# Hybrid attention/mLSTM trunk: the norm between the layers spread over ACT, POOL and DVE, the gates and the first unit of layer 1 run by blocks together, and the spill of x moved in the first stage

## What is computed

```python
for l in range(2):
    sh, sc, gt = split(silu(c) @ w_ada[l] + b_ada[l])         # adaLN, per sequence
    h = rmsnorm(x, g_pre[l]) * (1 + sc) + sh
    y = attention_branch(h) if l == 0 else mlstm_branch(h)     # both end in ... @ w_out
    x = x + gt * rmsnorm(y, g_post[l])
```

## Time and profile before

| | us |
|---|---|
| median of 3 runs | 2308.17 (2307.28 to 2312.15) |
| the profiled execution | 2304.96 |
| its span in the profile | 2303.4 |
| PE busy | 2189.6 |
| DVE busy | 951.0 |
| ACT busy | 687.5 |
| POOL busy | 65.2 |

### The profile page before, as it was taken

How to read it: one execution, slowest core, us unless ns; L and a number is a source line. 1 busy time by engine, 2 the same in 40 slices (tenths; PEclk the granted TensorE clock), 3 DMA queues, 4 the chain that set the end, 5 groups by cost and what they waited for, 6 DMA issues and landing times.

```text
span 2303.4 us, 40939 instructions
## 1 busy us (share of the span) xinstructions
PE 2189.6 (95%) x17200; PEld 1995.8 (87%) x17200; DVE 951.0 (41%) x1393; ACT 687.5 (30%) x1124; POOL 65.2 (3%) x108
## 2 busy tenths in 40 slices
PE   5889999999999999996999999999999999989996
PEld 3479998999999977784899999999999999977995
DVE  1423545636456421117543434334343434361225
ACT  2323443534344321123322222222222222232222
POOL 1000000000000000000000000000000000000000
PEclk9889999999999999997999999999999999999998
DMA  8983313222222399973356656784557568829522
GB/s 324 351 282 86 87 56 86 64 59 74 77 56 58 121 313 294 295 233 103 83 87 105 81 106 76 106 85 98 88 100 83 103 76 104 95 80 323 169 73 78
DMA packets 345741, 300.51 MB, mean 130 GB/s; under 512 B 8561, under 2 KB 287337, under 8 KB 344473
## 3 DMA queue, kind: packets, MB, share of 16 engines
q1 hardware_dynamic: 335952, 247.87, 48.5%
q0 software_dynamic: 9360, 50.19, 6.0%
q10 hardware_dynamic: 290, 0.32, 0.1%
HBM read 274.86 MB, written 27.56 MB: 131 GB/s over the span
## 4 chain that ended last, share of the span: by engine, by line
PE 88%; DVE 5%; DMA 2%; issue 2%; ACT 1%; SPq 1%; DVEq 0%; ACTq 0%
PE PJ L776 68%; PE MX L990 3%; DMA obuf<-in_w_ada 2%; PE MX L917 1%; PE MX L926 1%; PE MX L940 1%; PE PJ L797 1%; SPq L480 1%; DMA raw<-in_w_in_mlstm 1%; PE MX L1140 1%; PE MX L898 1%; PE MX L880 1%; PE MX L1096 1%; DVE arena L1615 1%; PE MX L1083 1%
## 5 line engine op out<-in xcount | busy, mean ns | idle before, releaser
L776 PE MATMUL PJ<-h_hi,w_hi 128*128 128x272 f32 x4320 | 925.1, 296 | 25.4 <-DVE h_lo L1653 12.5
L776 PE MATMUL PJ<-h_hi,w_lo 128*128 128x272 f32 x4320 | 898.1, 290 | 0.0
L776 PE MATMUL PJ<-h_lo,w_hi 128*128 128x272 f32 x4320 | 896.1, 289 | 0.8 <-issue 0.8
L776 PEld LDWEIGHTS PJ<-h_hi,w_hi 128*128 128x128 f32 x4320 | 681.5, 190 | 106.6 <-issue 88.5
L776 PEld LDWEIGHTS PJ<-h_lo,w_hi 128*128 128x128 f32 x4320 | 683.8, 190 | 1.0 <-issue 1.0
L776 PEld LDWEIGHTS PJ<-h_hi,w_lo 128*128 128x128 f32 x4320 | 679.8, 190 | 0.1
L1595 DVE TENSOR_TENSOR w_lo<-raw,w_hi 128x2048 fp32r<-128x2048 f32 x106 | 242.9, 2292 | 369.3 <-ACT w_hi L1213 369.1
L1213 ACT ACTIVATE w_hi<-raw 128x2048 fp32r<-128x2048 f32 x106 | 202.3, 1909 | 22.1 <-DMA raw<-in_w_in_mlstm 19.0
L1521 ACT ACTIVATE arena<-PJ 128x544 f32<-128x544 f32 x32 | 20.0, 625 | 238.2 <-PE PJ L776 238.1
L1913 DVE COPY modT<-MX 128x36 f32 x16 | 3.1, 196 | 210.8 <-PE MX L1001 210.8
L1891 DVE TENSOR_TENSOR w_lo<-raw,w_hi 128x2048 fp32r<-128x2048 f32 x30 | 68.8, 2293 | 36.2 <-ACT w_hi L1418 36.2
(11 more groups left out here) (331 smaller groups left out, 1827.5 us busy)
## 6 DMA issues: line engine op xcount, KB each, us to landing
arena<-in_w_ada SPq DMA_DIRECT2D x64, 1024.0 KB, 5.3
raw<-in_w_in_mlstm SPq DMA_DIRECT2D x64, 1024.0 KB, 14.5
raw<-in_w_in_attn SPq DMA_DIRECT2D x40, 1024.0 KB, 5.7
obuf<-in_w_ada SPq DMA_DIRECT2D x32, 1024.0 KB, 9.1
raw<-in_w_out_attn SPq DMA_DIRECT2D x16, 1024.0 KB, 7.9
raw<-in_w_out_mlstm SPq DMA_DIRECT2D x16, 1024.0 KB, 5.9
x_spill<-arena POOLq DMA_DIRECT2D x2, 4352.0 KB, 14.1
arena<-x_spill POOLq DMA_DIRECT2D x2, 4352.0 KB, 17.2
```

Source lines behind the costliest of these rows:

```text
L776: last = mm(PJ[:, 2 * pair + f, 0:HT], w, h[:, k, HT * f:HT * f + HT], start=(k == 0 and n == 0), stop=(k == KT - 1 and n == 2))
```

## The change

First stage: x is spilled behind the strips, after 29 of them are used, in two halves with semaphores of their own; the squares are added on DVE (as in the output products), and PE sums once after strip 11. `SQ_PARTS` goes.

Output products: their loops are written out. The gate product is made by ACT, in place in `obuf`, inside the output product (`gained`; blocks 0 to 3 at unit 6, 4 to 6 at unit 7, then one a unit). DVE's `gate_gain` moves to unit 5.

Residual: the product of y with `rB` is a plain product; 10 of 16 blocks (k mod 3 not 0) on POOL, 6 on DVE. DVE adds all 16.

Norm of layer 1: the product of x with `rB` is divided in the same way. ACT makes scale and shift in one pass (`full`) and the rounding in a second; DVE's low part is a plain subtraction. The sample columns are split ahead of the first scaling.

Gate and Q: PE takes blocks 0 to 11 of both units alternately, as h becomes ready, then blocks 12 to 15 of the gate and 12 to 15 of Q. Q's weights are rounded and split before the norm. x is spilled by a DMA from ACT's queue. The gate constants are loaded during the output product, `gates` comes at unit 0, `gate_maxima` and `gate_exps` at unit 1.

```diff
-SQ_PARTS = {(1, 1): range(0, 4), (1, 2): range(4, 8), (1, 3): range(8, 12), (2, 0): range(12, KT)}
+GAIN_AT = {6: range(0, 4), 7: range(4, 7), **{k: range(k - 1, k) for k in range(8, KT)}}
+ON_POOL = [k for k in range(KT) if k % 3]
+ON_DVE = [k for k in range(KT) if k % 3 == 0]
...
         def blocks_of(eng, ph, seg):
             k0, n, _ = seg
-            with eng.Fori(0, n // 2) as r:
-                for i in range(2):
-                    yield r, i, k0 + i
+            for i in range(n):
+                yield 0, i, k0 + i
...
 # POOL, first stage
             bias(1)
+            for a in range(2, 8):
+                bias(a)
             pool.wait_ge(xe_a, 10)
             pool.wait_ge(xe_d, 10)
-            pool.dma_start(x_spill, xflat).then_inc(spilled, 16)
-            for a in range(2, 8):
-                bias(a)
-            pool.wait_ge(spilled, 16)
+            pool.wait_ge(a0_used, 29)
+            for i in range(2):
+                cut = slice(KT // 2 * T * i, KT // 2 * T * (i + 1))
+                pool.dma_start(x_spill[:, cut], xflat[:, cut]).then_inc(spill0[i], 16)
+            pool.wait_ge(spill0[1], 16)
...
 # POOL, between the layers
-            pool.wait_ge(x_ready, KT)
-            pool.dma_start(x_spill, xflat).then_inc(spilled, 16)
-            pool.wait_ge(spilled, 32)
+            def scale_y(l):
+                pool.wait_ge(inv_done, 2 * l + 2)
+                for k in ON_POOL:
+                    pool.wait_ge(y_gained, KT * l + k + 1)
+                    pool.tensor_tensor(obuf[:, k, 0:TP], obuf[:, k, 0:TP], rB[:, 0:TP], ALU.mult)\
+                        .then_inc(y_scaled_p, 1)
+
+            scale_y(0)
+            pool.wait_ge(inv_done, 3)
+            for k in ON_POOL:
+                pool.wait_ge(x_ready, k + 1)
+                pool.tensor_tensor(obuf[:, k, 0:TP], xw[:, k, 0:TP], rB[:, 0:TP], ALU.mult).then_inc(x_scaled_p, 1)
...
 # PE, first stage
-                    if (e, j) in SQ_PARTS:
-                        sums(0, SQ_PARTS[e, j])
+                    if (e, j) == (2, 3):
+                        pe.wait_ge(sq_used, KT)
+                        for f in range(2):
+                            last = mm(MX[:, f, 0:HT], ones, rB[:, HT * f:HT * f + HT], start=True, stop=True)
+                        last.then_inc(s0_ready, 1)
...
 # PE, gate and Q
-            entry("gate", it0, 0, {}, 2 * KT)
+            def first(ph, k):
...
+                pe.wait_ge(h_ready, 2 * KT + k + 1)
...
+            for k in range(12):
+                first("gate", k)
+                first("l1", k)
+            for ph in ("gate", "l1"):
+                for k in range(12, KT):
+                    first(ph, k)
...
 # ACT, norm_split
+                def full(k):
+                    se, ks = (x_scaled_p, ON_POOL) if k in ON_POOL else (x_scaled_d, ON_DVE)
+                    act.wait_ge(se, count(ks, k))
+                    fn(obuf[:, k, 0:TP], obuf[:, k, 0:TP], ACT.Identity, bias=modT[:, 48 * l + k, 0:1],
+                       scale=modT[:, 48 * l + 16 + k, 0:1]).then_inc(hf_done, 1)
+
+                full(0)
+                for k in range(KT):
+                    if k + 1 < KT:
+                        full(k + 1)
+                    act.wait_ge(hf_done, k + 1)
+                    fn(h_hi[:, k, 0:TP], obuf[:, k, 0:TP], ACT.Copy).then_inc(hh_hi, 1)
...
 # ACT, output product and after
+                def gained(blocks):
+                    act.wait_ge(gain_done, l + 1)
+                    for b in blocks:
+                        act.wait_ge(freed["a"], FREED0["a"][ph] + b + 1)
+                        fn(obuf[:, b, 0:TP], obuf[:, b, 0:TP], ACT.Copy, scale=modT[:, 48 * l + 32 + b, 0:1])\
+                            .then_inc(y_gained, 1)
...
+                root(2 * l + 2)
+                gained(range(KT - 1, KT))
...
             out_product("out0")
-            root(2)
+            round_hi("l1", it0, 0)
             squares(2 * KT, x_from=0)
+            act.dma_start(x_spill, xflat).then_inc(spilled, 16)
             root(3)
             modulate(1, 1)
-            round_hi("l1", it0, 0)
...
 # DVE, residual (norm_split has the same order with scale(k) and low(k))
                 def scaled(k):
-                    stt(yk, yk, G[:, ds(k, 1), 0:1].rearrange("p a b -> p (a b)"), rB[:, 0:TP], ALU.mult, ALU.mult)\
-                        .then_inc(y_scaled, 1)
+                    dve.wait_ge(y_gained, KT * l + k + 1)
+                    tt(obuf[:, k, 0:TP], obuf[:, k, 0:TP], rB[:, 0:TP], ALU.mult).then_inc(y_scaled_d, 1)
                 def added(k):
+                    se, ks = (y_scaled_p, ON_POOL) if k in ON_POOL else (y_scaled_d, ON_DVE)
+                    dve.wait_ge(se, len(ks) * l + count(ks, k))
+                    tt(xw[:, k, 0:TP], xw[:, k, 0:TP], obuf[:, k, 0:TP], ALU.add).then_inc(x_ready, 1)
                 scaled(0)
-                scaled(1)
-                with dve.Fori(0, KT // 2 - 1) as r:
...
+                scaled(3)
+                for k in range(KT):
+                    if k + 6 in ON_DVE:
+                        scaled(k + 6)
+                    added(k)
...
             residual(0, 2)
+            split_lo("l1", it0, 0)
             dve.wait_ge(x_ready, KT)
             norm_split(1, 3)
-            split_lo("l1", it0, 0)
```

More of the change, by code:

```diff
@@ L86, with count @@
 STRIPS = 4
+GAIN_AT = {6: range(0, 4), 7: range(4, 7), **{k: range(k - 1, k) for k in range(8, KT)}}
+ON_POOL = [k for k in range(KT) if k % 3]
+ON_DVE = [k for k in range(KT) if k % 3 == 0]
+def count(blocks, k):
+    return sum(b <= k for b in blocks)
 RING = 4
@@ L1032, in _ @@
             sums(2 * KT)
-            entry("gate", it0, 0, {}, 2 * KT)
+            for ph in ("gate", "l1"):
+                pe.wait_ge(*freed_at(ph, it0, -2))
+                pe.wait_ge(lo_done, unit_no(ph, it0, 0) + 1)
+            pe.wait_ge(hs_ready, 5)
+            def first(ph, k):
+                s, pair = slot_of(ph, 0), pair_of(ph, 0)
+                pe.wait_ge(h_ready, 2 * KT + k + 1)
+                hi = w_hi[s][:, P * k:P * k + P]
+                lo = w_lo[s][:, P * k:P * k + P]
+                for n, (w, h) in enumerate(((hi, h_hi), (hi, h_lo), (lo, h_hi))):
+                    for f in range(2):
+                        last = mm(PJ[:, 2 * pair + f, 0:HT], w, h[:, k, HT * f:HT * f + HT],
+                                  start=(k == 0 and n == 0), stop=(k == KT - 1 and n == 2))
+                if k == KT - 1:
+                    last.then_inc(w_used, 1)
+            for k in range(12):
+                first("gate", k)
+                first("l1", k)
+            for ph in ("gate", "l1"):
+                for k in range(12, KT):
+                    first(ph, k)
             def gate_turn():
@@ L1144, in layer1 @@
             def layer1(it, prev):
-                for e in range(len(L1K)):
+                for e in range(1 if prev is None else 0, len(L1K)):
                     points = {}
@@ L1240, in modulate @@
                 act.wait_ge(A_ready, 4 + l)
-                with act.Fori(0, KT // 2) as r:
-                    for i in range(2):
-                        act.wait_ge(xs_done, r * 2 + (KT * l + i + 1))
-                        fn(h_hi[:, ds(r * 2 + i, 1), 0:TP].rearrange("p o t -> p (o t)"),
-                           obuf[:, ds(r * 2 + i, 1), 0:TP].rearrange("p o t -> p (o t)"), ACT.Identity,
-                           bias=modT[:, ds(r * 2 + (48 * l + i), 1), 0:1].rearrange("p a b -> p (a b)"))\
-                            .then_inc(hh_hi, 1)
+                def full(k):
[9 more added lines that the diff above has]
+                    fn(h_hi[:, k, 0:TP], obuf[:, k, 0:TP], ACT.Copy).then_inc(hh_hi, 1)
             def split_out(blocks):
@@ L1531, in layer1 @@
                         round_hi("l1", it, e + 1)
+                    if prev is None and e == 0:
+                        gates()
                     if prev is None and e == 1:
-                        gates()
-                    if prev is None and e == 2:
                         gate_exps()
@@ L1551, in _ @@
             out_product("out1", [(cs_out, 16 * MH)])
-            root(4)
             for n, (kg, t) in enumerate(PIECES):
@@ L1614, in inverse @@
                 dve.wait_ge(rt_ready, n)
-                chain(dve.reciprocal(rB, rB))
+                dve.reciprocal(rB, rB).then_inc(inv_done, 1)
+                dve.wait_ge(inv_done, n)
             def gain(l):
@@ L1720, in _ @@
             mod_empty("ada0", 0, 0)
+            chain(dve.memset(rB, 0.0))
+            for k in range(KT):
+                dve.wait_ge(sq_made, k + 1)
+                dve.wait_ge(sq_used, k)
+                tt(rB, rB, sqb[:, k % 2, :], ALU.add).then_inc(sq_used, 1)
+            mod_empty("ada0", 1, 1)
             mean_square(1)
```

91 lines of the change are left out of this document (45 added, 46 removed).

## The result

| | before | after |
|---|---|---|
| median, us | 2308.74 (2307.28 to 2312.15, 4 runs) | 2335.51 (2333.61 to 2338.88, 4 runs) |
| span of the profiled execution | 2303.4 | 2333.1 |

What follows compares the result with a forecast made beforehand. PE, busy 95%, was taken to bound the kernel, leaving three gaps to gain in: before, between and after the layers. Terms -10.5 + 0.3 + 1.5 + 0 = -8.7 us, put on the median, gave 2299.5 us; range 2284 to 2318.

Steps and rivals of the forecast that it cites:

- 0, bounds -1 and +1: Output products: writing out the loops costs 0 us, since no PE row waits on a loop there.
- Hold of 0.63 us: Residuals and norm: each POOL product shuts DVE out for 0.63 us, as long as DVE's own would last; chance 0.35.
- the prediction's own slope, 27 us for 1 us: Whole kernel: 1 us more hold of DVE per POOL product costs 27 us; the sign turns near 0.95 us.
- Rival (a), no disturbance: Residuals and norm: POOL and DVE do not disturb each other; sum -20.6 us, time 2287.6, chance 0.32.
- First stage, -10.5: Start to PE's full stretch: strips no longer queue behind the spill, -10.5 us; the norm comes 7.6 us earlier.
- Rival (c): First stage: late spill or norm gives back most of the gain, -3 instead of -10.5 us; 2307, chance 0.10.
- Norm and fused block: Between the layers, with holds: first block +4.3 us, PE's gate and Q 25.5 against 34.6, K's weights +2.8.
- the 2.8 bare for K's weights: After gate and Q: preparing K's weights takes 5.8 us from the gate's end, 2.8 of it not hidden.
- Gates earlier, +1.5: Layer 1: exponentials ahead of unit 3's rounding delay its weights 2.4 us, a 0.94 us wait goes: +1.5 us.
- the wait of about 2 us: Layer 1: the sign for the gates term, a PE wait of about 2 us ahead of unit 3.
- The end, 0: Last residual: 0 us with the holds, -6.3 us undisturbed; output copies keep up either way.

Runs made afterwards that it cites:

- changed kernel with no slow blocks: The changed kernel with every head of layer 1 reading the columns of head 1, which read fast there: 2312.72 us, ratio 1.0017.
- the kernel before with the columns of head 0: The kernel before with every head of layer 1 reading the weights of head 0: 2308.08 us.
- the pad: The changed kernel with eight more unused rows in the DRAM tensor that x is spilled to: 2335.75 us.
- run 1000: Not a label: "run" is a verb here, of PE's loops 1000 us later; the kernel before with PE's second output product written out took 2369.83 us.

## Why the prediction was wrong, by its own steps

**The blocks written out, "0, bounds -1 and +1".** This step failed, and on the kernel before it alone is worth 27 us. I asked whether a PE row waits on a loop. The effect works elsewhere: a longer program goes with slow reads of other column blocks of `w_in_mlstm`, in heads 0 and 4. No step of mine let the weights of layer 1 change speed, and no view of the kernel before that I read showed their slack. I had read that PE hardly waits inside the layers, and not that in head 3 all 16 DMA engines are busy for a whole load (window of the kernel before, columns as above):

```profile
1468.00:1486.00 18.00, 1.00 1.02 81
```

With heads 0 and 4 slow, 25 us of layer 1 are lost. The price is not the loops' alone: with PE's loops as loops again the changed kernel gains 9.6 us, or 15.5 with the products on DVE, and not 22.8, since heads 3 and 7 then take their turn at stalling.

**Hold of 0.63 us.** The mechanism is the one that the prediction named, and the term was mis-sized: the hold is 1.08 us. By the prediction's own slope, 27 us for 1 us, (1.08 - 0.63) x 27 = 12 us, which gives 2311.7. The changed kernel with no slow blocks takes 2312.7. That the two agree within 1 us is partly luck. In that kernel's profile the first residual starts 7.3 us earlier, where the forecast has 10.5, and from K's start to the last reciprocal it loses 5.3 us, where the forecast has 1.5. PE's waits don't show these 5.3 us (11.8 us in all, 12.5 before); its granted clock there is 0.96 to 0.99 by stretch, against 0.99 to 1.00. That execution lies 1.6 us above its median, and that of the kernel before 3.8 below. I had taken the nearest row, a DVE product, for a POOL product, which alone takes 1.21 us, twice as long.

**Rival (a), no disturbance.** Its condition is false, but its terms can be tested with all products on DVE. It had the mean square 0.7 earlier after the reciprocal and the first block 1.7 later behind it; that kernel has -1.0 and +1.6.

**First stage, -10.5.** The profile has -8.4, of which 6.9 arrive between the layers; with no slow blocks the medians say -8.1. The direction and the order were right (the strips gain more than the norm), the size was 2 too large. The norm came 4.6 us earlier and not 7.6, and behind it PE waits 9.9 us for ACT's copy, on the chain (5.0 for DVE before). PE's sums went from 20.1 us to 1.9, yet its waits from 34 us to the full stretch grew from 27.4 to 36.4: by these rows the strips set the pace in both kernels. No run has the moved spill without the new sums. Single profiles differ here, though: the kernel before with the columns of head 0, whose first stage is the same, enters the full stretch at 150.7, not at 154.35. Rival (c), that the gain is given back, came true in another place: not in the first stage, but in heads 3 and 7.

**Norm and fused block.** PE took 29.3 us to K, 28.3 by my step, with 2.70 of the 2.8 bare for K's weights. The step's sum was right. But the fusion's own share is only 3 us, since with Q's weights ready early the gate and then Q take 32.4, and not 34.6.

**Gates earlier, +1.5**: hidden behind the slow loads in the changed kernel. With the columns of head 1 PE waits 0.80 us ahead of unit 3, where before it waited 0.94 ahead of the gate transposes: the wait of about 2 us that was to show the term isn't there. **The end, 0**: +5.0, the same hold.

What stays open: why a program's length goes with the column blocks that read slowly. That the tensor's place in DRAM moves with the program would explain it, as would something else that goes with length; no run here shows an address, and the pad changed nothing. Nor do I know why 1.97, 2.05, 2.08 to 2.11 and 2.21 to 2.23 MB of instructions give 0, +33, +60 and +27 us, why heads 3 and 7 read up to a fifth slower once the first stage is changed, or whether a shorter program would be better than all of these.

## What to carry to other kernels

Before giving work to POOL beside a busy DVE, price a round of both: here a product that DVE makes in 0.6 us held it up for 1.08 us, so moving it was a loss. Where weights stream from DRAM within a slack of a few us, read the loads themselves (DMA share and GB/s inside one load, in every head) and not only PE's waits: time gained ahead of them can vanish in them. And treat writing out a loop as a change of its own with its own run, apart from the edits that need it.

## What I had not expected of the hardware

- Loads of 1 MB with the same shape, in packets of 512 bytes, ran at 53 to 144 GB/s in one kernel with the DMA engines busy throughout: 159 ns a packet against 55. Which column blocks are slow repeats every four heads, and it changed when loops of PE that run 1000 us later were written out.
- A POOL product of 128x512 took 1.21 us alone and 1.68 us beside DVE, whose instruction of the same size took 0.6 alone and 1.68 beside it.
- One kernel was 60 us slower, 2.7%, though every instruction up to the end of layer 1 was that of the kernel before; 49 of the 53 us of its profiled execution were lost by then.
